# Two joints of a transformer kernel in another order: weight splits and norm steps around a feed forward and a compressed projection

## The chip, the cores and the metric

The kernel is one program on one core of a Trainium2 chip. The metric is the device time of a whole launch in microseconds (us), the median of several runs. Beside the timed runs there is one profiled execution, and all times of single instructions come from it.

## The reference, cut to what matters

512 tokens of width 1024 go through two transformer blocks. All matmuls are in float32. What bears on the change:

```python
# first block: ... attention and gates give `merged`
mix_out = merged @ w_out                       # output product 1
h = h + rms_norm(mix_out, norm_mix_post)
n2 = rms_norm(h, norm_mlp_pre)
hid = square(relu(n2 @ w_up))                  # feed forward 1
h = h + rms_norm(hid @ w_down, norm_mlp_post)
# second block, layer 0: latent attention
hn = rms_norm(x, norm_mix[0])
cq = rms_norm(hn @ w_dq, q_norm)               # compressed queries, 384 wide
dkv = hn @ w_dkv                               # 256 compressed + 32 shared key columns
ckv = rms_norm(dkv[..., :256], kv_norm)
q = cq @ w_uq ; kv = ckv @ w_ukv               # then 16 heads of attention, w_o, feed forward 2
# layer 1: mLSTM mixer, w_o, feed forward 3
```

The two feed forwards and the output products of the second block have no norm behind them (`h = h + y`).

## The kernel before, in words

**Products in three passes.** Each float32 product is made of three matmuls in a reduced format (`mm3`, lines 82 to 84): hi*hi, hi*lo and lo*hi. So every operand is split into a hi part (ScalarE copies it to the narrower format) and a lo part (VectorE subtracts hi from the original).

**Weight units.** The weights come in units of up to 128x2048, in one fixed order (`plan_units`). A unit passes through two slots: SyncE loads it into `raw_weights` when VectorE has split the unit two before it (`load_unit`); ScalarE makes `weights_hi` (`split_hi`, L305, or `hi` in the feed forward, L1328) once it has landed and TensorE is through with the unit two before; VectorE makes `weights_lo` (`split_lo`, L311, or `lo`, L1423). TensorE waits for the lo part. The unit of a feed forward is 256 columns of `w_up` (two per step) or 512 of `w_down` (two per step), eight steps (`NF`); the compressed projections have three: 256 columns of the queries, the other 128 with 32 of the shared key, and 256 key-value columns.

**Order.** Nothing is scheduled by a planner. Each engine runs its queue in the order written in the code and waits on counting semaphores. The stages (`out_product`, `ffn`, `mla_down`, `mla`) follow each other without a barrier in one block.

**Norms.** The 512 tokens are four tiles of 128. Between two stages the residual is normed in two halves, tiles 0 and 1, then 2 and 3 (`norm_halves`). Per tile ScalarE sums squares (L962) and takes a root (L967); per half VectorE takes the reciprocal (L978) and scales the tiles (L981), TensorE transposes them (`turned`, L989, 16 transposes), ScalarE makes the hi part with the norm's gain from PSUM (L999, eight pieces of 128x256), VectorE the lo part (L1009). Where the product before has a norm behind it (`gain` given: output product 1 and feed forward 1), there is a second set of steps: VectorE adds the last partial product (L1467), ScalarE sums squares (L1380, or L1091 from PSUM) and takes roots (L1386, L1097), VectorE multiplies by the gain (L1470, or L1137) and updates the residual (`updated`, L1482, L1149). In these cases the next norm sums over the whole width at once (`whole=True`).

**The end of a feed forward on TensorE.** In the last step tokens 0 and 1 are finished in both column halves, then tokens 2 and 3; the first half's transposes stand ahead of the last group of matmuls. The next stage begins with the products of tiles 0 and 1 and has the second half's transposes a little later (in `ffn` behind `up_half(1, 0, 0)`, in `mla_down` behind `second(0)`).

**The compressed projections** (`mla_down`): TensorE makes unit one for tiles 0 and 1 (`first`), unit two for tile 0 (`second`), the transposes, then the rest; unit three for four tiles; and twelve transposes of the normed queries (L1588). ScalarE squares the query part from PSUM (L1602), splits units, squares the key-value part (L1609), makes the queries' hi (L1615); VectorE norms the queries (L1629), the key-values (L1638), and makes the queries' lo (L1642). The attention begins with a query product that waits for that lo.

## Time and profile before

| | before |
|---|---|
| median of 3 runs (lowest to highest) | 2203.77 us (2203.49 to 2205.46) |
| profiled execution, its own time | 2203.86 us |
| its span | 2202.1 us |
| TensorE busy (PE) | 2089.7 us, 95%, 11129 matmuls |
| VectorE busy (DVE) | 947.9 us, 43% |
| ScalarE busy (ACT) | 846.4 us, 38% |
| mean granted TensorE clock | 0.979 |

PE is TensorE's matmul queue, PEld its weight loads, DVE VectorE, ACT ScalarE, POOL GpSimd. Matmuls overlap, so the distance between their starts, not their length, is their price. A granted clock (PEclk) of 1.00 is the 2.4 GHz level, 0.50 the 1.2 GHz level. A row of a timeline is: start in us from the span's start, us until its end, engine, line, operation, what it writes and reads, the shape, the count of merged instructions, and in brackets how long the engine stood still just before and who ended that. Merged rows run from the first start to the last end.

### The profile page before, as it was taken

What the parts mean: (1) busy time and instruction counts of PE and PEld (TensorE: products, weight loads), DVE (VectorE), ACT (ScalarE), POOL (GpSimd) and SP (SyncE); (2) the same over time, 40 slices, a digit from 0 to 9 for tenths busy, and PEclk for the clock granted to TensorE, in tenths of its full rate; (3) what the DMA queues carried; (4) which work ended last, traced back from release to release, by engine and by line L of the source; (5) the groups of instructions that cost most, each with busy time, mean ns of one, the idle gap of its engine ahead of it and who ended that gap; (6) DMA issues with size and microseconds to landing.
All of it is one profiled execution on the core that took longest, in us unless ns stands there. A gap on an engine that the chain in (4) does not pass through costs nothing.

```text
span 2202.1 us, 26914 instructions
## 1 busy us (share of the span) xinstructions
PE 2089.7 (95%) x11129; PEld 1788.5 (81%) x11129; DVE 947.9 (43%) x1316; ACT 846.4 (38%) x1228; POOL 8.8 (0%) x20
## 2 busy tenths in 40 slices
PE   5799999999999999888889999999999999999999
PEld 5688888789888888686778988888877789888887
DVE  3545543334543344536554444334443344443343
ACT  3322332323533333536564433333454444333332
POOL 0000000000000000010000000000000000000000
PEclk9999999999999999988899999999999999999999
DMA  5232221223233333110011233223222212322322
GB/s 188 68 87 68 67 68 58 96 95 98 77 96 95 95 97 101 63 42 21 25 36 42 74 113 97 95 95 95 83 72 77 77 45 72 115 95 95 95 95 79
DMA packets 169800, 178.97 MB, mean 81 GB/s; under 512 B 6753, under 2 KB 139438, under 8 KB 169586
## 3 DMA queue, kind: packets, MB, share of 16 engines
q1 hardware_dynamic: 168280, 176.58, 25.5%
q8 instruction: 65, 1.06, 0.2%
q10 hardware_dynamic: 922, 1.09, 0.2%
q14 instruction: 21, 0.17, 0.0%
q0 software_dynamic: 512, 0.07, 0.0%
HBM read 174.50 MB, written 2.10 MB: 80 GB/s over the span
## 4 chain that ended last, share of the span: by engine, by line
PE 71%; DVE 6%; ACT 4%; issue 1%; ACTq 0%; DVEq 0%
PE psum L82 22%; PE psum L84 22%; PE psum L83 22%; DVE weights_lo L311 1%; PE psum L1790 1%; PE psum L1765 1%; PE psum L2177 1%; DVE weights_lo L1423 1%; PE psum L989 1%; ACT weights_hi L305 1%; PE psum L1780 1%; DVE scratch L1965 1%; ACT weights_hi L1328 0%; PE psum L1750 0%; ACT scratch L962 0%
## 5 line engine op out<-in xcount | busy, mean ns | idle before, releaser
L82 PE MATMUL psum<-norm_T_hi,weights_hi 128*128 128x512 f32 (+1 forms) x1440 | 540.4, 375 | 19.8 <-PEq L491 7.8
L84 PE MATMUL psum<-norm_T_hi,weights_lo 128*128 128x512 f32 (+1 forms) x1440 | 535.5, 372 | 0.0
L83 PE MATMUL psum<-norm_T_lo,weights_hi 128*128 128x512 f32 (+1 forms) x1440 | 535.3, 372 | 0.0
L82 PE MATMUL psum<-weights_hi,act_T_hi 128*128 128x512 f32 (+2 forms) x976 | 370.3, 379 | 14.8 <-DVE act_T_lo L1642 6.0
L84 PE MATMUL psum<-weights_hi,act_T_lo 128*128 128x512 f32 (+2 forms) x976 | 367.1, 376 | 0.0
L83 PE MATMUL psum<-weights_lo,act_T_hi 128*128 128x512 f32 (+2 forms) x976 | 367.1, 376 | 0.0
L82 PEld LDWEIGHTS psum<-norm_T_hi,weights_hi 128*128 128x128 f32 x1440 | 273.3, 190 | 70.3 <-issue 15.2
L84 PEld LDWEIGHTS psum<-norm_T_hi,weights_lo 128*128 128x128 f32 x1440 | 273.0, 190 | 46.9
L83 PEld LDWEIGHTS psum<-norm_T_lo,weights_hi 128*128 128x128 f32 x1440 | 273.4, 190 | 45.5
L1328 ACT ACTIVATE weights_hi<-raw_weights 128x2048 fp32r<-128x2048 f32 x93 | 177.5, 1909 | 342.2 <-PE psum L84 342.2
L1423 DVE TENSOR_TENSOR weights_lo<-raw_weights,weights_hi 128x2048 fp32r<-128x2048 f32 x93 | 213.2, 2293 | 106.7 <-ACT weights_hi L1328 106.7
L311 DVE TENSOR_TENSOR weights_lo<-raw_weights,weights_hi 128x2048 fp32r<-128x2048 f32 (+3 forms) x74 | 156.2, 2112 | 181.9 <-ACT weights_hi L305 179.2
L82 PEld LDWEIGHTS psum<-weights_hi,act_T_hi 128*128 128x128 f32 x976 | 186.8, 191 | 49.7 <-issue 7.2
L84 PEld LDWEIGHTS psum<-weights_hi,act_T_lo 128*128 128x128 f32 x976 | 186.5, 191 | 31.4
L83 PEld LDWEIGHTS psum<-weights_lo,act_T_hi 128*128 128x128 f32 x976 | 186.9, 191 | 30.8
L82 PE MATMUL psum<-weights_hi,norm_T_hi 128*128 128x256 f32 (+2 forms) x672 | 194.3, 289 | 17.0 <-DVE weights_lo L311 9.2
L1431 DVE TENSOR_TENSOR act_T_lo<-scratch,act_T_hi 128x512 fp32r<-128x512 f32 x96 | 66.4, 692 | 323.9 <-ACT act_T_hi L1339 323.9
L83 PE MATMUL psum<-weights_lo,norm_T_hi 128*128 128x256 f32 (+2 forms) x672 | 191.7, 285 | 0.0
L84 PE MATMUL psum<-weights_hi,norm_T_lo 128*128 128x256 f32 (+2 forms) x672 | 191.6, 285 | 0.0
L305 ACT ACTIVATE weights_hi<-raw_weights 128x2048 fp32r<-128x2048 f32 (+3 forms) x74 | 130.9, 1769 | 101.0 <-PE psum L84 90.4
L1335 ACT ACTIVATE scratch<-psum 128x512 f32<-128x512 f32 x96 | 57.5, 599 | 278.5 <-PE psum L84 278.5
L82 PEld LDWEIGHTS psum<-weights_hi,norm_T_hi 128*128 128x128 f32 x672 | 132.0, 196 | 20.1 <-DVE weights_lo L311 10.0
(256 smaller groups left out, 1958.7 us busy)
## 6 DMA issues: line engine op xcount, KB each, us to landing
raw_weights<-in_ffn_w_dram SPq DMA_DIRECT2D x64, 1024.0 KB, 5.2
raw_weights<-in_w_in_dram SPq DMA_DIRECT2D x36, 512.0 KB, 4.2
raw_weights<-in_w_up_dram SPq DMA_DIRECT2D x16, 1024.0 KB, 5.6
raw_weights<-in_w_down_dram SPq DMA_DIRECT2D x16, 1024.0 KB, 4.9
raw_weights<-in_w_in_dram SPq DMA_DIRECT2D x12, 1024.0 KB, 5.1
raw_weights<-in_mlstm_w_in_dram SPq DMA_DIRECT2D x8, 1024.0 KB, 5.2
raw_weights<-in_w_out_dram SPq DMA_DIRECT2D x4, 1024.0 KB, 5.4
raw_weights<-in_mla_w_o_dram SPq DMA_DIRECT2D x4, 1024.0 KB, 5.8
```

Of the source, the lines that this page charges most:

```text
L82: pe.matmul(out, ah, bh, start=start, stop=False)
L83: pe.matmul(out, ah, bl, start=False, stop=False)
L84: return pe.matmul(out, al, bh, start=False, stop=stop)
L305: act.activation(WH[:, u % 2, 0:c], RAW[:, u % 2, 0:c], ACT.Copy).then_inc(w_hi, 1)
L311: dve.tensor_tensor(WL[:, u % 2, 0:c], RAW[:, u % 2, 0:c], WH[:, u % 2, 0:c].bitcast(F32), SUB).then_inc(w_lo, 1)
L989: mm = pe.transpose(PS[:, bank, q * P:q * P + P], XN[:, t, k * P:k * P + P], IDENT[:, :])
L1328: act.activation(WH[:, u % 2, :], RAW[:, u % 2, :], ACT.Copy).then_inc(w_hi, 1)
L1335: act.activation(HS[:, f, :], PS[:, up_banks[f], :], ACT.Relu).then_inc(fr.sem, 1)
L1423: dve.tensor_tensor(WL[:, u % 2, :], RAW[:, u % 2, :], WH[:, u % 2, :].bitcast(F32), SUB).then_inc(w_lo, 1)
L1431: dve.tensor_tensor(AL[:, f, :], HS[:, f, :], AH[:, f, :].bitcast(F32), SUB).then_inc(fl.sem, 1)
L1765: pe.matmul(PS[:, b, c:c + w], QT[:, n % 2, t * P:t * P + P], KT[:, n % 2, 0:w], start=True, stop=True).then_inc(sc.sem, 1)
L1780: mm = pe.transpose(PS[:, 3 + q % 2, (i % 4) * P:(i % 4) * P + P], SB[:, i * P:i * P + P], IDENT[:, :])
```

## The change

Only the two stages with a gain and their successors change their order: output product 1 into feed forward 1, and feed forward 1 into the compressed projections.

- `normed` leaves tile 3 out where `whole` is set; a new step `normed_last` scales it on ScalarE, and `turned` waits for both.
- At the end of `out_product` with a gain, the split of the feed forward's second unit stands behind `updated(1)` and `rooted(3)`; `ffn` no longer has it (`whole_in`). On ScalarE that is the same place, on VectorE it is ahead of `normed`.
- At the end of `ffn` with a gain, ScalarE splits the next unit and makes the first half's hi pieces ahead of all squares of tiles 2 and 3; VectorE does the lo part and the lo pieces ahead of the multiplies, and splits the unit after it behind `updated(1)`.
- In `mla_down`, unit three is split ahead of the four squares of the query part; TensorE's twelve transposes of the queries move ahead of the last token tile of unit three; the hi and lo of the queries move ahead of the squares of tiles 2 and 3 and of the key-values' norm.
- A parameter `ahead=0` of `out_product`, three unused or new semaphores, and a count are bookkeeping.

```diff
@@ norm_halves @@
                     for t in (2 * h, 2 * h + 1):
-                        dve.tensor_scalar(XN[:, t, :], X[:, t, :], rstd[:, t:t + 1], None, MUL).then_inc(xnc.sem, 1)
+                        if not (whole and t == 3):
+                            dve.tensor_scalar(XN[:, t, :], X[:, t, :], rstd[:, t:t + 1], None, MUL).then_inc(xnc.sem, 1)
+
+                @staticmethod
+                def normed_last(act):
+                    act.wait_ge(rsc.sem, rsc.at(2))
+                    act.activation(XN[:, 3, :], X[:, 3, :], ACT.Copy, scale=rstd[:, 3:4]).then_inc(xlc.sem, 1)
 
                 @staticmethod
                 def turned(pe, h):
-                    pe.wait_ge(xnc.sem, xnc.at(2 * h + 2))
+                    pe.wait_ge(xnc.sem, xnc.at(3 if whole and h else 2 * h + 2))
+                    if whole and h:
+                        pe.wait_ge(xlc.sem, xlc.at(1))
                     for b, bank in enumerate((banks_a, banks_b)[h]):
@@ out_product, scalar @@
                     rooted(3)
+                    split_hi(act, u0 + 5)
                 else:
@@ out_product, vector @@
                     updated(1)
+                    split_lo(dve, u0 + 5)
                 else:
@@ ffn, scalar @@
                 if whole_in:
-                    hi(act, 0, 0)
                     for t in (2, 3):
                         came_in(t)
                         norm.last_sum(act, t)
+                    norm.normed_last(act)
                 else:
@@ ffn, scalar @@
                         nxt.last_sum(act, t)
+                    split_hi(act, u0 + 4 * NF)
+                    nxt.hi(act, 0)
                     squared(0, 2)
-                    split_hi(act, u0 + 4 * NF)
                     squared(0, 3)
                     squared(1, 2)
                     rooted(2)
-                    nxt.hi(act, 0)
                     squared(1, 3)
                     rooted(3)
+                    split_hi(act, u0 + 4 * NF + 1)
                 elif nxt:
@@ ffn, vector @@
                 norm.normed(dve, 1)
-                lo(dve, 0, 0)
+                if not whole_in:
+                    lo(dve, 0, 0)
                 norm.lo(dve, 1)
@@ ffn, vector @@
                     dve.wait_ge(stage_ld.sem, stage_ld.at(16))
-                    for h in range(2):
-                        t = 2 * h
-                        add(0, t)
-                        add(0, t + 1)
-                        if h:
-                            split_lo(dve, u0 + 4 * NF)
-                        for b in range(2):
-                            if b:
-                                add(1, t)
-                                if h:
-                                    nxt.lo(dve, 0)
-                                add(1, t + 1)
-                            dve.wait_ge(acc.sem, acc.at(8 * (NF - 1) + added[b][t + 1]))
-                            scaled(b, t)
-                            scaled(b, t + 1)
-                            if b == 0:
-                                mean(h)
-                        updated(h)
-                        if h == 0:
-                            nxt.normed(dve, 0)
+                    def landed(b, t):
+                        dve.wait_ge(acc.sem, acc.at(8 * (NF - 1) + added[b][t]))
+                        scaled(b, t)
+
+                    add(0, 0)
+                    add(0, 1)
+                    landed(0, 0)
+                    landed(0, 1)
+                    mean(0)
+                    add(1, 0)
+                    add(1, 1)
+                    landed(1, 0)
+                    landed(1, 1)
+                    updated(0)
+                    nxt.normed(dve, 0)
+                    add(0, 2)
+                    add(0, 3)
+                    split_lo(dve, u0 + 4 * NF)
+                    nxt.lo(dve, 0)
+                    landed(0, 2)
+                    landed(0, 3)
+                    mean(1)
+                    add(1, 2)
+                    add(1, 3)
+                    landed(1, 2)
+                    landed(1, 3)
+                    updated(1)
+                    split_lo(dve, u0 + 4 * NF + 1)
                 else:
@@ mla_down @@
                 for t in range(NT):
+                    if t == 3:
+                        pe.wait_ge(xn.sem, xn.at(NT))
+                        for k in range(3):
+                            for q in range(NT):
+                                mm = pe.transpose(PS[:, banks[k], q * P:q * P + P], CQ[:, q, k * P:k * P + P], IDENT[:, :])
+                            mm.then_inc(tp.sem, 1)
                     group_N(pe, u0 + 2, 0, 256, 256, KD,
...
-                pe.wait_ge(xn.sem, xn.at(NT))
-                for k in range(3):
...
             @block.scalar
             def _(act):
-                split_hi(act, u0 + 1)
+                def squared(t):
...
                 for t in (2, 3):
                     act.wait_ge(res_in.sem, res_in.at(t + 1))
                     norm.last_sum(act, t)
+                norm.normed_last(act)
                 norm.hi(act, 1)
+                split_hi(act, u0 + 2)
                 for t in range(NT):
                     act.wait_ge(gemm, cq_done[t])
-                    if t == 2:
-                        split_hi(act, u0 + 2)
...
                 split_hi(act, u0 + 3)
-                for t in range(NT):
...
-                act.wait_ge(ms.sem, ms.at(2))
-                act.activation(root[:, 4:8], m0[:, 4:8], ACT.Sqrt).then_inc(rt.sem, 1)
+                squared(0)
+                squared(1)
                 for k in range(3):
...
+                squared(2)
+                squared(3)
+                act.wait_ge(ms.sem, ms.at(2))
+                act.activation(root[:, 4:8], m0[:, 4:8], ACT.Sqrt).then_inc(rt.sem, 1)
...
             def _(dve):
                 norm.normed(dve, 1)
-                split_lo(dve, u0 + 1)
                 norm.lo(dve, 1)
+                split_lo(dve, u0 + 2)
                 dve.wait_ge(sq.sem, sq.at(4))
                 dve.tensor_scalar(m0[:, 0:4], s0[:, 0:4], 1.0 / QR, EPS, MUL, ADD).then_inc(ms.sem, 1)
-                split_lo(dve, u0 + 2)
                 dve.wait_ge(rt.sem, rt.at(1))
...
+                split_lo(dve, u0 + 3)
+                for k in range(3):
+                    dve.wait_ge(th.sem, th.at(k + 1))
+                    dve.scalar_tensor_tensor(in_place(AL[:, k, :]), by_tile(PS[:, banks[k], :]), col(C_MISC, k),
...
                 dve.wait_ge(sq.sem, sq.at(8))
...
-                split_lo(dve, u0 + 3)
...
-                for k in range(3):
-                    dve.wait_ge(th.sem, th.at(k + 1))
...
```

VectorE, from output product 1 into feed forward 1 (L1149 or L1161 the residual update, L1423 or L314 the lo part of unit 1, L981 or L985 the scaled tiles, L1009 or L1020 the transposed norm's lo). Before:

```order
L1149 SCALAR_TENSOR_TENSOR residual<-scratch,small,residual 128x1024 x2
L1426 UNCONDITIONAL_BRANCH
L978 RECIPROCAL small<-small 128x2
L981 TENSOR_SCALAR scratch<-residual,small 128x1024 x2
L1423 TENSOR_TENSOR weights_lo<-raw_weights,weights_hi 128x2048
L1009 SCALAR_TENSOR_TENSOR norm_T_lo<-psum,gain_columns,norm_T_hi 128x256 x8
```

Now:

```order
L1161 SCALAR_TENSOR_TENSOR residual<-scratch,small,residual 128x1024 x2
L314 TENSOR_TENSOR weights_lo<-raw_weights,weights_hi 128x2048
L1440 UNCONDITIONAL_BRANCH
L981 RECIPROCAL small<-small 128x2
L985 TENSOR_SCALAR scratch<-residual,small 128x1024
L1020 SCALAR_TENSOR_TENSOR norm_T_lo<-psum,gain_columns,norm_T_hi 128x256 x8
```

The lo part of the unit moved from behind the scaled tiles to right behind the update, and one scaled tile is gone.

ScalarE, end of feed forward 1 (L967 or L970 the next norm's root, L1380 or L1393 the squares, L305 or L308 the hi part of the next unit, L999 or L1010 the transposed norm's hi). Before:

```order
L967 ACTIVATE small<-small 128x1
L1380 ACTIVATE scratch,small<-scratch 128x512
L305 ACTIVATE weights_hi<-raw_weights 128x2048
L1380 ACTIVATE scratch,small<-scratch 128x512 x2
L1386 ACTIVATE small<-small 128x1
L999 ACTIVATE norm_T_hi<-psum,gain_columns 128x256 x8
L1380 ACTIVATE scratch,small<-scratch 128x512
L1386 ACTIVATE small<-small 128x1
```

Now:

```order
L970 ACTIVATE small<-small 128x1
L308 ACTIVATE weights_hi<-raw_weights 128x2048
L1010 ACTIVATE norm_T_hi<-psum,gain_columns 128x256 x8
L1393 ACTIVATE scratch,small<-scratch 128x512 x3
L1399 ACTIVATE small<-small 128x1
L1393 ACTIVATE scratch,small<-scratch 128x512
L1399 ACTIVATE small<-small 128x1
L308 ACTIVATE weights_hi<-raw_weights 128x1280
```

The split and the eight hi pieces stand ahead of all four squares of tiles 2 and 3.

ScalarE in the compressed projections (L1602 or L1630 squares of the query part, L1609 or L1619 of the key-value part, L1615 or L1639 the queries' hi). Before:

```order
L999 ACTIVATE norm_T_hi<-psum,gain_columns 128x256 x8
L1602 ACTIVATE scratch,small<-psum 128x384 x2
L305 ACTIVATE weights_hi<-raw_weights 128x2048
L1602 ACTIVATE scratch,small<-psum 128x384 x2
L1605 ACTIVATE small<-small 128x4
L305 ACTIVATE weights_hi<-raw_weights 128x1152
L1609 ACTIVATE scratch,small<-psum 128x256 x4
L1612 ACTIVATE small<-small 128x4
L1615 ACTIVATE act_T_hi<-psum,gain_columns 128x4x128 x3
```

Now:

```order
L990 ACTIVATE scratch<-residual,small 128x1024
L1010 ACTIVATE norm_T_hi<-psum,gain_columns 128x256 x8
L308 ACTIVATE weights_hi<-raw_weights 128x2048
L1630 ACTIVATE scratch,small<-psum 128x384 x4
L1633 ACTIVATE small<-small 128x4
L308 ACTIVATE weights_hi<-raw_weights 128x1152
L1619 ACTIVATE scratch,small<-psum 128x256 x2
L1639 ACTIVATE act_T_hi<-psum,gain_columns 128x4x128 x3
L1619 ACTIVATE scratch,small<-psum 128x256 x2
L1643 ACTIVATE small<-small 128x4
```

The 2048-wide split stands ahead of all squares, the queries' hi between the two pairs of key-value squares, and the scaled tile (L990) ahead of the hi pieces.

## Rows read from the trace of the kernel before

**Rows 1.** Waits over the span: total us, times, longest us
```profile
PE psum L82 <- DVE weights_lo L311: 16.3, 10, 4.2
```

**Rows 2.** Timeline of TensorE, joint A: start, us, instruction, idle time before
```profile
568.78 0.58 PE L82 MATMUL psum<-norm_T_hi,weights_hi 128*128 128x256 f32 x1 [4.86 <-DVE weights_lo L1423]
...
573.89 1.91 PE L989 MATMUL psum<-ident,scratch 128*128 128x128 f32 x16
575.56 0.36 PE L82 MATMUL psum<-norm_T_hi,weights_hi 128*128 128x256 f32 x1
...
590.57 0.50 PE L82 MATMUL psum<-weights_hi,act_T_hi 128*128 128x512 f32 x1 [0.39 <-DVE weights_lo L1423]
```

**Rows 3.** Timelines of ScalarE and VectorE, joint A
```profile
559.75 1.90 ACT L1328 ACTIVATE weights_hi<-raw_weights 128x2048 fp32r<-128x2048 f32 x1
...
564.90 0.17 DVE L978 RECIPROCAL small<-small 128x2 f32<-128x2 f32 x1 [1.72 <-ACT small L967]
...
566.44 2.29 DVE L1423 TENSOR_TENSOR weights_lo<-raw_weights,weights_hi 128x2048 fp32r<-128x2048 f32 x1
```

**Rows 4.** Stretches: busy PE, PEld, DVE, ACT, POOL; PEclk; DMA share; GB/s
```profile
514.00:516.00 2.00, 0.53 (x4) 0.53 (x5) 1.42 (x1) 0.00 (x0) 0.00 (x0) 1.00 0.00 0
...
925.00:929.00 4.00, 3.37 (x17) 3.40 (x18) 3.97 (x10) 2.30 (x6) 0.00 (x0) 0.57 0.13 44
...
937.00:945.00 8.00, 7.86 (x37) 7.87 (x38) 0.77 (x3) 1.55 (x4) 0.00 (x0) 0.50 0.30 76
```

**Rows 5.** ScalarE's groups by shape: busy us, mean ns, idle us before
```profile
L436 ACT ACTIVATE scratch<-residual,small 128x1024 f32<-128x1024 f32 x2 | 2.2, 1140 | 0.2 <-DVE small L450 0.2
```

**Rows 6.** Timeline of TensorE, stretch B
```profile
925.63 0.55 PE L82 MATMUL psum<-weights_hi,norm_T_hi 128*128 128x256 f32 x1 [5.44 <-DVE norm_T_lo L1009]
...
937.14 0.50 PE L82 MATMUL psum<-weights_hi,norm_T_hi 128*128 128x160 f32 x1 [4.21 <-DVE weights_lo L311]
...
962.71 0.56 PE L82 MATMUL psum<-weights_hi,norm_T_hi 128*128 128x256 f32 x1 [3.07 <-DVE weights_lo L311]
...
983.25 0.69 PE L82 MATMUL psum<-weights_hi,act_T_hi 128*128 128x384 f32 x1 [5.95 <-DVE act_T_lo L1642]
...
988.83 0.42 PE L82 MATMUL psum<-weights_hi,act_T_hi 128*128 128x384 f32 x1
...
992.16 0.47 PE L82 MATMUL psum<-weights_hi,act_T_hi 128*128 128x512 f32 x1
```

**Rows 7.** Timeline of ScalarE, stretch B
```profile
913.46 0.30 ACT L967 ACTIVATE small<-small 128x1 f32<-128x1 f32 x1
...
916.67 1.90 ACT L305 ACTIVATE weights_hi<-raw_weights 128x2048 fp32r<-128x2048 f32 x1
...
923.75 3.01 ACT L999 ACTIVATE norm_T_hi<-psum,gain_columns 128x256 fp32r<-128x256 f32 x8
...
957.00 1.92 ACT L305 ACTIVATE weights_hi<-raw_weights 128x2048 fp32r<-128x2048 f32 x1 [7.84 <-PE psum L84]
```

**Rows 8.** Timeline of VectorE, stretch B
```profile
918.60 2.29 DVE L311 TENSOR_TENSOR weights_lo<-raw_weights,weights_hi 128x2048 fp32r<-128x2048 f32 x1 [2.00 <-ACT weights_hi L305]
...
924.61 3.23 DVE L1009 SCALAR_TENSOR_TENSOR norm_T_lo<-psum,gain_columns,norm_T_hi 128x256 fp32r<-128x256 f32 x8 [1.84 <-ACT norm_T_hi L999]
...
928.47 1.29 DVE L1470 TENSOR_TENSOR scratch<-scratch 128x512 f32<-128x512 f32 x2
...
929.87 2.48 DVE L1482 SCALAR_TENSOR_TENSOR residual<-scratch,small,residual 128x1024 f32<-128x1024 f32 x2
...
935.60 1.49 DVE L311 TENSOR_TENSOR weights_lo<-raw_weights,weights_hi 128x1280 fp32r<-128x1280 f32 x1
```

**Rows 9.** Timelines of three engines: compressed queries turned and split
```profile
975.83 1.47 PE L1588 MATMUL psum<-ident,scratch 128*128 128x128 f32 x12
...
977.22 3.02 ACT L1615 ACTIVATE act_T_hi<-psum,gain_columns 128x512 fp32r<-128x512 f32 x3
...
980.03 3.17 DVE L1642 SCALAR_TENSOR_TENSOR act_T_lo<-psum,gain_columns,act_T_hi 128x512 fp32r<-128x512 f32 x3
```

More of the change, by code:

```diff
@@ L282, in build @@
         gate = count("gate_rows")
+        oth = count("head_pairs_hi")
+        qsc = count("query_scales")
+        n_xl = count("norm_last_scaled")
         drained = count("heads_gated")
@@ L403, in _ @@
                     dve.tensor_copy(COLS[:, :, :].rearrange("p a k -> p (a k)")[:, 0:NCOL], PS[:, 0, 0:NCOL]).then_inc(v1.sem, 1)
-            param.passed(32)
+            param.passed(32); cleared.passed(1)
             stage_ld.passed(10 * 16)
@@ L1027, in halves, with out_product @@
             return x[:, t, 512 * b:512 * b + 512]
-        def out_product(block, name, gain, banks, nxt, srch, srcl, ready, early, freed=None):
+        def out_product(block, name, gain, banks, nxt, srch, srcl, ready, early, freed=None, ahead=0):
             u0 = at[name]
@@ L1098, in rooted @@
                                    bias=pm[:, t:t + 1]).then_inc(qr.sem, 1)
-                for j in range(3):
+                for j in range(ahead, 3):
                     split_hi(act, u0 + j + 1)
@@ L1154, in add @@
                     dve.tensor_tensor(x, psum(b, t), x, ADD).then_inc(res.sem, 1)
-                for j in range(3):
+                for j in range(ahead, 3):
                     split_lo(dve, u0 + j + 1)
```

16 lines of the change are left out of this document (6 added, 10 removed).

## The prediction

> **What bounds the kernel.** I read the table of engines and the slices first: TensorE is busy for nearly the whole span, VectorE and ScalarE for less than half. So ScalarE's and VectorE's work costs nothing by itself; it counts only where TensorE stands still for it. The list of waits for TensorE is the second view: on top stands VectorE's lo half of a weight unit (L311), 16.3 us in ten waits, the longest 4.2 [rows 1]. Third, the timelines of the three engines at the places that the diff touches. There are two: the joint from the first output product into the first feed forward (554 to 592 us, joint A), and the stretch from the end of that feed forward through the compressed projections into the latent attention (900 to 1000 us, stretch B). Everything else keeps its order: `ahead` is given by no call and stays 0, and the other output products and feed forwards go through the `gain is None` and `whole=False` paths. No matmul, split or DMA is added or removed.
>
> **Joint A.** TensorE stood still for 4.86 us, until 568.78, when the lo half of feed forward unit 1 was ready [rows 2]. On VectorE [rows 3] that split (2.29, from 566.44) stood behind the residual update, which ended at 564.90 - 1.72 = 563.18, a wait of 1.72 for ScalarE's root, the reciprocal and two scaled tiles (565.07 to 566.44, 0.7 each). Its hi half had been there since 559.75 + 1.90 = 561.65. Now it comes right behind the update: 563.15 + 2.29 = 565.4. TensorE resumes 3.35 us earlier.
>
> The second gain is the clock. The 24 matmuls behind the old wait took 573.89 - 568.78 = 5.11 us, 0.213 each; the 120 behind the transposes took 590.57 - 575.56 less a gap of 0.39, so 0.122 each [rows 2]. The granted clock was 0.50, the 1.2 GHz level, behind such waits [rows 4]. The wait that is left is 563.92 to 565.4, 1.5 us. From 514 to 516 TensorE stood still for as long (busy 0.53 of 2.00) and the clock was granted at 1.00 [rows 4]; so I take the 2.4 GHz level: 24 x 0.122 = 2.93, 2.2 us less. Sum: 5.5 us.
>
> What takes the place of the old wait? The transposes need all four normed tiles. The reciprocal now starts at 565.45, tile 2 is scaled by VectorE, tile 3 by ScalarE at 1.14 us [rows 5], the price of the same operation elsewhere in the kernel against 0.7 on VectorE, side by side: ready at 566.9. TensorE comes for them at 565.4 + 2.9 = 568.3. Hidden by 1.4 us; were that cover gone, the cost would be what lies over it, 0 to 1.14 us.
>
> **Stretch B, first unit.** Four waits lie here [rows 6]: 5.44, 4.21, 3.07 and 5.95 us. Before the first, ScalarE split the unit's hi half from 916.67, behind a square that waited for VectorE [rows 7], and made the eight transposed hi pieces only after two more squares, one more wait, a square and a root, from 923.75. Now the split follows the root that ends at 913.76. It may start then: its source is long landed, and the products that still need its slot end near 913 (24 matmuls of 512 columns, near 0.23 each, and 16 transposes lie between them and TensorE's stop at 920.19). So hi ends at 915.7. VectorE is free for lo at 918.60 - 2.00 = 916.60 [rows 8] and ends it at 918.9. The hi pieces take 3.01 us from about 916.1, as soon as the first bank is transposed; the lo pieces 3.23 us from 918.9 to 922.1, a pair each 0.81 us. TensorE is free at 925.63 - 5.44 = 920.19, finds the first pair (919.7), and uses a pair in 6 x 0.122 = 0.73 us. The wait of 5.44 is gone and 48 matmuls end at 926.0.
>
> **Second unit.** Its lo half started at 935.60, behind the update of tiles 2 and 3 (929.87) and two scaled tiles [rows 8]. The update depends on squares and sums that now come after the lo pieces: VectorE has two multiplies, a mean, two adds, two multiplies, six passes of 0.65 (two took 1.29) and the two small ones at 0.16 [rows 8], so 4.3 us: update from 926.4 to 928.9 instead of 929.87 to 932.35. ScalarE's four squares and two roots interleave and end with it. The split follows directly (1.49): TensorE's second unit starts at 930.4 instead of 937.14, **6.75 us** earlier. A wait of 926.0 to 930.4 = 4.4 us remains, as long as the old one, and I let it cost what the old one did: half level through 24 matmuls and 16 transposes, to about 945.6 [rows 4]. ScalarE's scaled tile is ready before these 24 matmuls end, as in A.
>
> **Third unit.** ScalarE started its hi half at 957.00, held by the wait for the third token tile's product. It now stands first and waits only for the fourth tile of unit one, 24 matmuls of 2.7 us earlier, near 954.3 in the old times: hi 956.2, lo (2.29) 958.5, before TensorE's old stop at 959.64. So the wait of **3.07** goes. The squares of the query part move behind it by up to 1.9 us; they were done long before they are needed. With no stop there, the slow start goes too: 96 matmuls took 975.83 - 962.71 = 13.12 us, at 0.122 each 11.7: **1.4 us**.
>
> **Into the attention.** The twelve transposes of the compressed queries now stand ahead of the last 24 matmuls of the unit. Before, TensorE ended them at 977.30 and stood until 983.25 for hi (3.02) and lo (3.17, from 980.03) [rows 9]. Now, in new times, the unit starts at 959.64 - 6.75 = 952.9, the transposes are reached after 72 x 0.122 = 8.8 at 961.7, take 1.35, and the last product ends at 966.0. Queries are normed by 956.9 (squares 953.6, mean, root, reciprocal, four tiles 2.6), 4.8 us of cover. Hi runs from 962.3, lo from 963.35 to 966.5. The query product starts at 966.55 against 983.25, 16.7 us earlier in all. Of the 5.95 us wait 0.6 remains, and the clock need not fall: 18 matmuls and 8 transposes took 988.83 - 983.25 = 5.58; the next 18 took 992.16 - 988.83 = 3.33 [rows 6], so with 0.8 for the transposes 4.13: **1.45 us**. Sum of B: 18.15.
>
> Behind that all engines keep their distances. Sixteen small copies of the shared key part start with the transposes, some 14.5 us earlier, and VectorE wants them 18 us earlier; that could hold VectorE for about a microsecond, in front of a 3.6 us idle stretch before its next split. I cost it at nothing; without that cover it is 0 to 1 us.
>
> Total: 5.5 + 18.15 = **23.7 us**. The profiled execution took 2203.86 (span 2202.10, 1.76 around it), so 2180.2; the median of the runs is 0.09 lower, so I say 2180.1.
>
> The clock is where a page bears on it. The Trainium skill, TensorE: Matmul & The Clock Gate, Part 1, says that the gate is checked on a free-running rhythm, so the same kernel can meet it at another phase. By that rule the 4.4 us wait may or may not be followed by the lower level, and the sum would be that of the first rival below where it is not. The trace bears out both: behind the 5.44 us wait the half level lasted only to about 928.7 (0.57 from 925 to 929), behind the shorter one of 4.21 it held 8 us [rows 4].
>
> **Rivals.**
> 1. The clock stays up over the second unit. 24 matmuls at 0.11 to 0.12 instead of 0.213 give 2.4, 16 transposes 575.56 - 573.89 = 1.67 [rows 2] instead of the 3.3 left of the 8.4 another 1.6: 4.0 more, 2176.1. For it: the 5.44 us wait was nearly over before the level fell. Against: the matmuls behind the other four long waits, 4.86, 4.21, 3.07 and 5.95, all started slow. Chance 0.14.
> 2. The third unit's hi half comes too late after all, since ScalarE waits in front of its squares. The 3.07 stays with its slow start (1.4) and the slow query product (1.45): 5.9 less, 2186.0. The margin is 1.1 us. Chance 0.12.
> 3. The diff acts only on paths that TensorE does not feel, or the attention behind takes the gain back (shared keys, its own waits): 2204. Against it, TensorE names these very steps as releasers. Chance 0.02.
> 4. Slower: the half level, once met at the second unit, does not end. After it, 120 matmuls would cost 0.096 more each (11.5), 96 another 0.091 (8.7), the transposes and the 18 query matmuls 3.7: 23.9, all of the gain. Six more groups at this level, 24 key-value matmuls at 0.43 for 0.23 and 18 queries, add 7: 2211. It decides from about 24 us lost, near 45 us of unbroken half level; the longest here, behind the 4.21, ended soon after 945. Chance 0.02.
>
> **Numbers.** Forecast 0.70, rivals as above. A measurement of this kernel can tell 0.2% (4.4 us) from no change. Forecast and rivals 1 and 2 are faster: 0.96; same 0.02; slower 0.02. The range takes in the first two rivals with their own errors, 2 us either way for the clock in the attention: 2174 to 2188.
>
> **What would show it.** In the new profile: a wait of about 1.5 us in place of 4.86 in joint A and no lower clock behind it; no wait ahead of the first compressed unit, about 4.4 ahead of the second, none ahead of the third; under 1 us ahead of the query product. ScalarE scales two tiles of 128x1024 more, VectorE two fewer. I am wrong if the waits shrink and the time does not, or if new waits on the scaled tiles or on the squares show at TensorE's transposes.

## The result and the profile after

| | before | after |
|---|---|---|
| median (lowest to highest) | 2203.63 us (2203.41 to 2205.46) | 2183.05 us (2181.51 to 2183.6) |
| span of the profiled execution | 2202.1 us | 2180.9 us |
| mean granted TensorE clock | 0.979 | 0.979 |

The ratio is 0.9903, 95% interval 0.989 to 0.9915: 20.6 us less. The forecast was 2180.1 us, 23.7 less. The time lies inside the range, 3 us off. Where these 3 us are is what most of the runs below ask. One execution of run 1 below took 2381.16 us at a granted clock of 0.838 and is left out of that run's figures.

**Joint A.** TensorE of the changed kernel, beside [rows 2]:

```profile
565.35 0.39 PE L82 MATMUL psum<-norm_T_hi,weights_hi 128*128 128x256 f32 x1 [1.53 <-DVE weights_lo L314]
...
568.33 1.91 PE L1000 MATMUL psum<-ident,scratch 128*128 128x128 f32 x16
569.99 0.36 PE L82 MATMUL psum<-norm_T_hi,weights_hi 128*128 128x256 f32 x1
...
585.01 0.50 PE L82 MATMUL psum<-weights_hi,act_T_hi 128*128 128x512 f32 x1 [0.39 <-DVE weights_lo L1437]
```

The wait is 1.53 us in place of 4.86, and the 24 matmuls behind it took 568.33 - 565.35 = 2.98 us in place of 5.11. VectorE and ScalarE, beside [rows 3], show why: the split (L314) now comes ahead of the reciprocal (L981), and tiles 2 and 3 are scaled side by side, the one on VectorE (L985), the other on ScalarE (L990), both done by 566.55, 1.8 us before TensorE comes for them. On the spot that is 3.33 + 2.13 = 5.5 us; the new kernel stood 0.1 us ahead already when its wait began (563.82 for 563.92).

```profile
563.01 2.28 DVE L314 TENSOR_TENSOR weights_lo<-raw_weights,weights_hi 128x2048 fp32r<-128x2048 f32 x1
565.21 0.15 DVE L981 RECIPROCAL small<-small 128x2 f32<-128x2 f32 x1
565.40 0.75 DVE L985 TENSOR_SCALAR scratch<-residual,small 128x1024 f32<-128x1024 f32 x1
```
```profile
565.40 1.15 ACT L990 ACTIVATE scratch<-residual,small 128x1024 f32<-128x1024 f32 x1 [0.62 <-DVE small L981]
```

**Stretch B.** TensorE, beside [rows 6] and the transposes of [rows 9]; the first row, the first unit's first matmul, has no wait:

```profile
914.34 0.28 PE L82 MATMUL psum<-weights_hi,norm_T_hi 128*128 128x256 f32 x1
...
924.33 0.34 PE L82 MATMUL psum<-weights_hi,norm_T_hi 128*128 128x160 f32 x1 [4.07 <-DVE weights_lo L314]
...
932.02 0.32 PE L82 MATMUL psum<-weights_hi,norm_T_hi 128*128 128x160 f32 x1
...
954.53 1.47 PE L1610 MATMUL psum<-ident,scratch 128*128 128x128 f32 x12
...
959.74 0.44 PE L82 MATMUL psum<-weights_hi,act_T_hi 128*128 128x384 f32 x1 [0.86 <-DVE act_T_lo L1661]
```

From 932.02 up to the wait of 0.86 us that ends at 959.74 TensorE has no wait at all; unit three starts inside, at 945.87. VectorE in the same stretch, beside [rows 8]: the split of unit one and the lo pieces run without a pause, and the split of unit two follows the update directly.

```profile
910.84 2.28 DVE L314 TENSOR_TENSOR weights_lo<-raw_weights,weights_hi 128x2048 fp32r<-128x2048 f32 x1
913.04 3.22 DVE L1020 SCALAR_TENSOR_TENSOR norm_T_lo<-psum,gain_columns,norm_T_hi 128x256 fp32r<-128x256 f32 x8
...
920.39 2.48 DVE L1497 SCALAR_TENSOR_TENSOR residual<-scratch,small,residual 128x1024 f32<-128x1024 f32 x2
922.79 1.49 DVE L314 TENSOR_TENSOR weights_lo<-raw_weights,weights_hi 128x1280 fp32r<-128x1280 f32 x1
```

**What came later.** The same matmul starts this much earlier in the changed kernel (start before less start after): second unit 937.14 - 924.33 = 12.8 us, third 962.71 - 945.87 = 16.8, query product 983.25 - 959.74 = 23.5, first matmul of the second query product, behind the first key-value product, 1001.16 - 976.12 = 25.0. At the end of the span it is 21.2. So 3.8 us of what stood at 976 us were handed back behind it, in stages whose code and order are the same. Matching matmuls tell where. At the last transposes of the attention, ahead of the output product, the lead is still 24.7:

```profile
1199.57 0.63 PE L1755 MATMUL psum<-ident,scratch 128*128 128x128 f32 x4 [0.68 <-DVE scratch L1975]
```
```profile
1174.92 0.63 PE L1782 MATMUL psum<-ident,scratch 128*128 128x128 f32 x4 [0.68 <-DVE scratch L2002]
```

In feed forward 2 it is 22.9 (1266.76 and 1243.88), in the mixer 21.7 (1705.58 and 1683.84), at output product 3 21.2 (1804.92 and 1783.75). The stretches show the clock there. Before (busy PE, PEld, DVE, ACT, POOL; PEclk; DMA share; GB/s):

```profile
1036.00:1056.00 20.00, 17.51 (x82) 14.23 (x83) 14.53 (x39) 10.19 (x23) 0.00 (x0) 0.66 0.10 31
1088.00:1108.00 20.00, 17.47 (x84) 14.38 (x85) 14.60 (x39) 10.38 (x24) 0.00 (x0) 0.66 0.17 54
1136.00:1160.00 24.00, 16.53 (x97) 13.77 (x98) 16.48 (x42) 14.02 (x30) 0.00 (x0) 0.86 0.00 1
1196.00:1208.00 12.00, 9.41 (x66) 8.80 (x66) 4.76 (x4) 4.31 (x3) 0.00 (x0) 0.86 0.15 46
1628.00:1640.00 12.00, 9.08 (x41) 6.98 (x42) 6.17 (x6) 5.54 (x7) 0.00 (x0) 0.86 0.61 176
1780.00:1796.00 16.00, 12.58 (x68) 10.81 (x67) 8.51 (x21) 5.90 (x14) 0.00 (x0) 0.89 0.00 0
```

After, the same six places of the program:

```profile
1008.00:1028.00 20.00, 16.16 (x57) 13.01 (x58) 13.34 (x30) 9.24 (x19) 0.00 (x0) 0.57 0.09 29
1060.00:1080.00 20.00, 17.02 (x65) 13.87 (x66) 13.31 (x31) 9.35 (x20) 0.00 (x0) 0.57 0.15 53
1112.00:1136.00 24.00, 21.71 (x100) 17.91 (x101) 16.27 (x41) 13.50 (x29) 0.00 (x0) 0.64 0.00 1
1176.00:1188.00 12.00, 10.00 (x60) 9.73 (x61) 5.28 (x3) 3.89 (x3) 0.00 (x0) 0.72 0.52 164
1604.00:1616.00 12.00, 8.47 (x31) 6.48 (x30) 7.39 (x7) 6.13 (x7) 0.00 (x0) 0.72 0.50 142
1756.00:1772.00 16.00, 12.58 (x53) 9.97 (x52) 8.45 (x24) 7.11 (x11) 0.00 (x0) 0.79 0.00 1
```

In all six the granted clock is lower than before. The first three lie in the attention, where it costs next to nothing in this profile, 0.4 us: TensorE waits there for VectorE in any case (for the rotation of queries and keys), and a slower approach only shortens that wait. The waits from 1000 to 1160 us show it, in one line of before and one of after (total, times, longest):

```profile
PE psum L1750 <- DVE scratch L1955: 8.6, 3, 5.3
```
```profile
PE psum L1777 <- DVE scratch L1982: 3.2, 3, 1.1
```

The last three lie at the start of output product 2, early in the mixer behind feed forward 2, and late in the mixer, where less covers it. 12 us at 0.72 in place of 0.86 is 1.7 us of clock more, 16 at 0.79 in place of 0.89 is 1.6: 5.0 in the three. The leads above fall by 1.8, 1.0 and 0.5 us around them, 3.3 in all, so the waits inside them cover the rest. The mean clock of the whole is 0.979 in both kernels: the change took four waits away and did not lessen the share of the lower level; that share moved.

### The profile page after: what moved, and what is told of

Same layout as the page of the kernel before. It is cut to its first block, busy times and chain, and to the rows that moved or that the text cites. A ratio compares the mean times of both kernels' runs of the same rounds, so it can differ in the third digit from the quotient of the medians.

```text
span 2180.9 us, 26916 instructions
## 1 busy us (share of the span) xinstructions
PE 2091.1 (96%) x11129; PEld 1789.5 (82%) x11129; DVE 946.2 (43%) x1314; ACT 848.9 (39%) x1230; POOL 8.8 (0%) x20
## 4 chain that ended last, share of the span: by engine, by line
PE 71%; DVE 6%; ACT 3%; issue 1%; ACTq 0%; DVEq 0%
PE psum L82 22%; PE psum L84 22%; PE psum L83 22%; DVE weights_lo L314 1%; PE psum L1817 1%; PE psum L1792 1%; PE psum L2204 1%; PE psum L1807 1%; DVE weights_lo L1437 1%; PE psum L1000 1%; DVE scratch L1992 1%; ACT weights_hi L308 0%; ACT weights_hi L1341 0%; PE psum L1777 0%; PE psum L2183 0%
## 5 line engine op out<-in xcount | busy, mean ns | idle before, releaser
L314 DVE TENSOR_TENSOR weights_lo<-raw_weights,weights_hi 128x2048 fp32r<-128x2048 f32 (+1 forms) x75 | 158.5, 2114 | 189.7 <-ACT weights_hi L308 187.0
L308 ACT ACTIVATE weights_hi<-raw_weights 128x2048 fp32r<-128x2048 f32 (+1 forms) x75 | 132.8, 1770 | 102.8 <-PE psum L84 92.0
```

Of the source, the lines that this page charges most:

```text
L308: act.activation(WH[:, u % 2, 0:c], RAW[:, u % 2, 0:c], ACT.Copy).then_inc(w_hi, 1)
L314: dve.tensor_tensor(WL[:, u % 2, 0:c], RAW[:, u % 2, 0:c], WH[:, u % 2, 0:c].bitcast(F32), SUB).then_inc(w_lo, 1)
```

## The experiments

All are compared with runs of the kernel before on the same chip; each gives its ratio with 95% interval.

**1. Joint A alone.** The end of the feed forward and the compressed projections are in the order of before; against the changed kernel:

```diff
@@ ffn, scalar @@
-                    split_hi(act, u0 + 4 * NF)
-                    nxt.hi(act, 0)
                     squared(0, 2)
+                    split_hi(act, u0 + 4 * NF)
                     squared(0, 3)
                     squared(1, 2)
                     rooted(2)
+                    nxt.hi(act, 0)
                     squared(1, 3)
                     rooted(3)
-                    split_hi(act, u0 + 4 * NF + 1)
...
@@ mla_down, vector @@
                 norm.normed(dve, 1)
+                split_lo(dve, u0 + 1)
                 norm.lo(dve, 1)
...
```

VectorE's end of the feed forward, unit three and the queries' transposes, hi and lo go back in the same way.

> The order of joint A alone (the end of output product 1 into the feed forward), with tile 3 of both norms still scaled by ScalarE; everything behind it in the order of before. Forecast's theory: the wait ahead of the second unit's matmuls shrinks from 4.86 to 1.5 us and the 24 matmuls behind it take 2.9 in place of 5.1 us, so 5.5 us less than before: 2198.1. Rival, the wait shrinks but the matmuls stay at the lower level: 3.3 less, 2200.3. Second rival, the gain is handed back at the clock's lower stretches further on, as some 4 us of the full change were: 2 to 6 us less, with joint A itself 5.5.

Measured: 2198.45 for 2204.33, ratio 0.9969 (0.9958 to 0.998): 5.9 less by the medians, 4.4 to 9.3 by the interval. The seven runs spread from 2194.45 to 2201.06, so this agrees with the 5.5 forecast and does not measure it to half a us. TensorE does:

```profile
566.63 0.39 PE L82 MATMUL psum<-norm_T_hi,weights_hi 128*128 128x256 f32 x1 [1.54 <-DVE weights_lo L314]
...
569.61 1.91 PE L1000 MATMUL psum<-ident,scratch 128*128 128x128 f32 x16
```

Wait 1.54, and 2.98 us for the 24 matmuls, as in the changed kernel: both halves of this term stand. The run also keeps tile 3 on ScalarE in the second norm, which takes 0.6 us off the wait ahead of the second compressed unit (3.62 for 4.21); so it is joint A and a little more. From the second query product, where it is 4.5 us ahead of before, to the end, where it is 4.4, it hands nothing back.

**2. The change without joint A.**

```diff
@@ out_product, scalar and vector @@
                     rooted(3)
-                    split_hi(act, u0 + 5)
...
                     updated(1)
-                    split_lo(dve, u0 + 5)
@@ ffn, scalar and vector @@
                 if whole_in:
+                    hi(act, 0, 0)
...
-                if not whole_in:
-                    lo(dve, 0, 0)
+                lo(dve, 0, 0)
```

> The whole change without joint A: the split of the feed forward's second unit is back behind the norm. Theory: wait of 4.86 us and the slow 24 matmuls are back, 5.5 us more than the changed kernel, 2188.6, and 15.1 less than before. If the two parts add up, this gain and that of joint A alone make the 20.6 of the whole; if the clock's phase takes a share of its own, they do not, by up to 4 us.

Measured: 2186.8 for 2204.33, ratio 0.9922 (0.9908 to 0.9935): 3.8 more than the changed kernel's 2183.05, 3.4 more than run 3 on the same chip, not 5.5. The expectation had forgotten that tile 3 stays on ScalarE. The split stands behind the scaled tiles again, so it gains what VectorE no longer does, 0.65 us, and this time the lower level ended inside the 24 matmuls (4.33 us for 5.11). Wait and matmuls together are 4.0 us longer than in the changed kernel:

```profile
567.73 0.58 PE L82 MATMUL psum<-norm_T_hi,weights_hi 128*128 128x256 f32 x1 [4.21 <-DVE weights_lo L1436]
...
572.06 1.91 PE L1000 MATMUL psum<-ident,scratch 128*128 128x128 f32 x16
```

**3. Tile 3 on VectorE.** Both calls of `normed_last` and the wait for it are gone:

```diff
@@ norm_halves @@
-                        if not (whole and t == 3):
-                            dve.tensor_scalar(XN[:, t, :], X[:, t, :], rstd[:, t:t + 1], None, MUL).then_inc(xnc.sem, 1)
+                        dve.tensor_scalar(XN[:, t, :], X[:, t, :], rstd[:, t:t + 1], None, MUL).then_inc(xnc.sem, 1)
```

> The changed kernel with tile 3 of both norms scaled by VectorE as before. Theory: the tile is wanted only 1.4 us (joint A) and more (stretch B) after it is ready in either way, so no change at the joints: 2183.0, within 0.5. Rival: the transposes wait for VectorE, 0.3 to 0.7 us at each joint, up to 1.4 us more.

Measured: 2183.45 for 2204.33, ratio 0.9905 (0.989 to 0.992); no difference from the changed kernel, and its transposes in joint A have no wait. Where the split comes ahead of the norm, moving the tile gains nothing; where it stands behind it, as in run 2, it shortens the wait by 0.65.

**4. The changed kernel once more.**

> The changed kernel once more, unaltered, with a profile of its own. If the stretches of lower clock hang on what TensorE did before them, all twelve come at the same places to 4 us and the span repeats to 0.5 us. If they hang on something that runs beside the kernel, single stretches are longer, shorter or absent, and the runs spread by steps of 1 to 3 us at a granted clock from 0.978 to 0.985.

Measured: 2183.23 for 2203.3, ratio 0.9907 (0.9891 to 0.9922). The profiled span is 2182.5, 1.6 longer than the first, and stretches have changed their clock. Two of them, 0.86 and 1.00 here; in the first profile 1176 to 1188 stood at 0.72, and in 1136 to 1160 the level was full:

```profile
1136.00:1160.00 24.00, 22.15 (x130) 17.54 (x128) 10.51 (x38) 12.89 (x35) 0.00 (x0) 0.86 0.13 45
1176.00:1188.00 12.00, 8.18 (x67) 7.66 (x66) 5.70 (x4) 4.31 (x3) 0.00 (x0) 1.00 0.19 60
```

So the clock of a stretch is not fixed by the program alone. The Trainium skill, TensorE: Matmul & The Clock Gate, Part 1, has the gate checked on a free-running rhythm; the two profiles agree, 0.72 and 1.00 in one stretch of one program. They don't explain the 3 us by chance, though: none of the eight runs of the changed kernel came under 2181.5.

The same 4 us are handed back here, but elsewhere. The second query product starts at 977.50, 23.7 us ahead of before, and at the end of the attention the lead is only 20.4:

```profile
1179.14 0.63 PE L1782 MATMUL psum<-ident,scratch 128*128 128x128 f32 x4 [0.68 <-DVE scratch L2002]
```

So 3.2 us went inside the attention, in its last part, where TensorE no longer waits for VectorE: from 1138 to 1146 the clock is 0.57, and in the same part of the first profile, 1137 to 1145, it is 1.00. Behind that only 0.8 more is lost.

**5. The compressed queries last.** Transposes, hi and lo stand where they stood before; of ScalarE's part:

```diff
@@ mla_down, scalar @@
                 squared(0)
                 squared(1)
-                for k in range(3):
-                    act.wait_ge(tp.sem, tp.at(k + 1))
-                    act.activation(in_place(AH[:, k, :]), ...)
                 squared(2)
                 squared(3)
                 act.wait_ge(ms.sem, ms.at(2))
                 act.activation(root[:, 4:8], m0[:, 4:8], ACT.Sqrt).then_inc(rt.sem, 1)
+                for k in range(3):
+                    act.wait_ge(tp.sem, tp.at(k + 1))
+                    act.activation(in_place(AH[:, k, :]), ...)
```

> The changed kernel with the compressed queries' transposes back behind the last token tile of unit three, and their hi and lo back behind the key-values' norm. Theory: the wait ahead of the query product goes from 0.86 back to 5.95 us and the 18 matmuls behind it start at the lower level: 5.1 + 1.45 = 6.6 more than the changed kernel, 2189.6. Rival, the attention behind has slack and hands some back: 2 to 4 more. The clock further on may add or take 2.

Measured: 2189.66 for 2203.3, ratio 0.9936 (0.9923 to 0.995): 6.4 more than the changed kernel's 2183.23 on the same chip. The wait ahead of the query product is 5.94 again. The term, 5.1 + 1.45, is right in the time.

**6. Unit three late.**

```diff
@@ mla_down, scalar @@
                 norm.hi(act, 1)
-                split_hi(act, u0 + 2)
                 for t in range(NT):
                     act.wait_ge(gemm, cq_done[t])
+                    if t == 2:
+                        split_hi(act, u0 + 2)
@@ mla_down, vector @@
                 norm.lo(dve, 1)
-                split_lo(dve, u0 + 2)
                 dve.wait_ge(sq.sem, sq.at(4))
                 dve.tensor_scalar(m0[:, 0:4], ...)
+                split_lo(dve, u0 + 2)
```

> The changed kernel with unit three's split back between the squares of the query part. Theory: the wait of 3.07 us ahead of unit three and its slow start of 1.4 are back: 4.5 more than the changed kernel, 2187.5. Rival: with the second unit early the hi half finds its product done and half of the wait stays away: 1.5 to 2.5 more, 2185.

Measured: 2184.01 for 2203.3, ratio 0.9913 (0.9898 to 0.9928): 0.8 more than the changed kernel, and its four runs, 2183.53 to 2185.02, overlap with that one's. Yet the wait is back in full:

```profile
949.35 0.58 PE L82 MATMUL psum<-weights_hi,norm_T_hi 128*128 128x256 f32 x1 [3.07 <-DVE weights_lo L314]
```

From the second unit's start (923.85) to the query product (964.71) it takes 40.86 us, in the repeat of run 4 36.40 (924.73 to 961.13): 4.5 us more. What was lost by 965 came back behind it: the clock of the three stretches in the attention is higher than in the first profile, the waits for VectorE there are long again, and the stretch at 1176 is at 0.86 (0.72).

```profile
1008.00:1028.00 20.00, 16.05 (x77) 12.35 (x78) 15.31 (x40) 11.95 (x26) 0.00 (x0) 0.74 0.00 0
1060.00:1080.00 20.00, 15.27 (x69) 11.17 (x69) 14.77 (x32) 12.37 (x26) 0.00 (x0) 0.72 0.00 1
1112.00:1136.00 24.00, 16.18 (x96) 13.48 (x95) 16.11 (x41) 14.25 (x31) 0.00 (x0) 0.86 0.00 1
1176.00:1188.00 12.00, 9.41 (x67) 8.80 (x66) 5.05 (x4) 4.31 (x3) 0.00 (x0) 0.86 0.19 56
```
```profile
PE psum L1778 <- DVE scratch L1983: 8.4, 3, 5.3
```

Its mean clock is 0.982, the changed kernel's 0.978 and 0.979: 0.003 to 0.004 of 2182 us, 6.5 to 8.7 us of full clock less lost. How far each profile is ahead of before, in us, shows that this kernel hands nothing back (the profiles differ from that of before by up to 1.2 us ahead of joint A already, so what counts is the change along a row):

| profile | second query product | end of the attention | feed forward 2 | span |
|---|---|---|---|---|
| changed kernel | 25.0 | 24.7 | 22.9 | 21.2 |
| changed kernel, run 4 | 23.7 | 20.4 | 20.5 | 19.6 |
| unit three late, run 6 | 20.1 | 20.3 | 20.3 | 20.3 |
| joint A alone, run 1 | 4.5 | 4.5 | 4.4 | 4.4 |

So this term of the forecast was right at its place, 4.5 us, and worth 0.8 in the whole.

**7 and 8. Work added.** Every transpose of the compressed queries is made twice, or three times, into the same place:

```diff
                         for k in range(3):
-                            for q in range(NT):
+                            for q in list(range(NT)) * 2:
```

> The changed kernel with every one of the twelve transposes of the compressed queries made twice, into the same place: work of 1.35 us more on TensorE near 955 us, nothing else altered. It moves all that follows by 1.35 us. Theory, the 3.9 us that the changed kernel loses behind 1176 us are a matter of where the lower clock falls: the time changes by something else than 1.35, and the stretches near 1180, 1610 and 1765 us are of another length. Rival, they are a fixed cost of the change: 1.35 more, 2184.4, with the same stretches.

> As the kernel with every one of the twelve transposes made twice, but three times: 2.7 us more of TensorE's work near 955 us. Work made twice had cost nothing that could be measured (2183.0 for 2183.2). If the delay is added to the end, 2185.9; if what follows is set by where the lower clock falls among VectorE's own waits in the attention, anything from 2182 to 2187, and the stretches there are of another length.

Measured: 2183.0 for 2203.3, ratio 0.9906 (0.9891 to 0.9921), and 2182.8 for 2204.72, ratio 0.9902 (0.9887 to 0.9917). Neither 1.35 nor 2.7 us of TensorE's time shows in the whole. Half of the expectation was wrong: the wait of 0.86 us ahead of the query product took the first part of the delay, so that this started only 0.5 and 1.4 us later than in the repeat of run 4 (961.67 and 962.52 for 961.13). The rest went with the clock: with three times, the stretch from 976 to 984 is at 1.00, where the repeat has 0.79:

```profile
976.00:984.00 8.00, 4.85 (x28) 4.88 (x29) 6.27 (x6) 5.04 (x8) 0.00 (x0) 1.00 0.37 89
```

Of the matmuls of the second query product, the first starts 1.65 us later than in the repeat (979.15 for 977.50), the seventeenth 0.1 (982.02 for 981.93). With two times, the attention takes the delay: behind it, at the wait shown in run 4, this kernel stands at 1179.18, the repeat at 1179.14. The rival, a fixed cost that a delay adds to, falls.

**9. The end of the feed forward back.** The part of run 1's diff that concerns `ffn` and the second unit's split in `mla_down`, on both engines, with unit three and the queries left as changed.

> The changed kernel with the end of feed forward 1 and the second unit's split back in the order of before; joint A, unit three and the queries stay changed. Theory: the waits of 5.44 ahead of the first and 4.21 ahead of the second compressed unit are back; the changed kernel's TensorE stood 8.0 us further ahead behind these two than ahead of them, so 8 more, 2191.2. Rival, from what undoing unit three cost (0.9 where 4.5 was forecast): the attention hides part of the lower clock behind VectorE's waits of its own, and only 4 to 5 us come through, 2188.

Measured: 2188.67 for 2204.72, ratio 0.9931 (0.9917 to 0.9945): 5.4 to 5.6 more than the changed kernel's medians on other chips; counted as 16.1 less than before, where the changed kernel had 20.6 and 20.1, only 4.0 to 4.5. That is nearer to the rival's number than to the theory's. TensorE:

```profile
919.48 0.55 PE L82 MATMUL psum<-weights_hi,norm_T_hi 128*128 128x256 f32 x1 [5.44 <-DVE norm_T_lo L1020]
...
930.32 0.34 PE L82 MATMUL psum<-weights_hi,norm_T_hi 128*128 128x160 f32 x1 [2.85 <-DVE weights_lo L314]
```

From the transposes ahead of the first unit (909.31) to the second unit it takes 21.0 us, in the changed kernel 14.5 (909.86 to 924.33): 6.5 more, not 8. Of 4.21 us of wait 2.85 are back. VectorE scales one tile less ahead of the split, 0.7, and the 48 matmuls between the waits were slower, 8.0 us for 7.3, inside the time that VectorE needs. The spans differ by 5.8, and this profile was 0.5 ahead at those transposes, so 6.3 of the 6.5 are there at the end: that the attention hides a part, the rival's reason, is not what this profile shows. The theory failed already ahead of the attention.

**10 and 11. One step further.** The second unit's split no longer waits for the update of tiles 2 and 3, and the transposes that do are behind both tiles of that unit:

```diff
@@ ffn, scalar @@
                     squared(0, 3)
+                    split_hi(act, u0 + 4 * NF + 1)
                     squared(1, 2)
...
-                    split_hi(act, u0 + 4 * NF + 1)
@@ ffn, vector @@
                     nxt.lo(dve, 0)
+                    split_lo(dve, u0 + 4 * NF + 1)
...
                     updated(1)
-                    split_lo(dve, u0 + 4 * NF + 1)
@@ mla_down, tensor @@
                 second(0)
-                norm.turned(pe, 1)
                 second(1)
+                norm.turned(pe, 1)
```

> A step further than the change: the compressed projections' second unit is split ahead of the multiplies and the update of tiles 2 and 3 (hi half between ScalarE's squares, lo half right behind the lo pieces), and TensorE takes the transposes of tiles 2 and 3 behind second(1) instead of behind second(0). Theory: the wait of 4.07 us ahead of the second unit goes; in its place TensorE waits for the normed tiles 2 and 3, near 927.0, reaching them at 925.5, 1.5 us; some 3 to 5 us less than the changed kernel, 2178 to 2180. Rival: the update falls behind by the 1.5 us of the split and ScalarE's squares by another 1.4, so that the transposes wait 3 us or more and only 1 us or less is gained: 2182. It would be slower if the third unit's squares came late in turn.

> The kernel with the second unit split early once more, beside the next one on the same chip: 2177.3 as before, within 1.5.

Measured: 2177.32 for 2204.33, ratio 0.9873 (0.9858 to 0.9888), and again 2174.84 for 2204.72, ratio 0.9865 (0.9849 to 0.988). It beats both kernels, the changed one by 6 to 8 us.

```profile
927.87 2.84 PE L1000 MATMUL psum<-ident,scratch 128*128 128x128 f32 x16 [1.89 <-ACT scratch L990]
```

One wait of 1.89 in place of one of 4.07, and 2.84 us for the 16 transposes behind it, so at the lower level; the query product starts at 956.18 for 959.74, 3.6 us earlier. The rest goes with the clock: single runs lie at 2173.65 to 2179.42, those with a mean clock of 0.984 or 0.985 under 2175.5, those with 0.980 or 0.981 over 2178.5. Both profiles, spans 2177.6 and 2176.9 at 0.980, are of the longest runs, so where the shorter ones save is not shown.

**12. The transposes of the queries ahead of tile 2.** In run 10's kernel `if t == 3` becomes `if t == 2`.

> The kernel with the second unit split early, and the twelve transposes of the compressed queries ahead of the third token tile of unit three instead of the fourth. Theory: the normed queries are there 1.7 us before TensorE comes for them, hi and lo lie under 48 matmuls instead of 24, and the wait of 0.86 us ahead of the query product goes: 0.9 less, 2176.4. Rival: the normed queries are late and TensorE waits at the transposes for up to 0.9 us instead, no change; or the gain vanishes in the attention, as the 1.35 us of added work did.

Measured: 2176.99 for 2204.72, ratio 0.9875 (0.986 to 0.989), beside 0.9865 (0.9849 to 0.988) for run 11 on the same chip: no gain that can be told, though the wait of 0.86 is gone and the query product starts at 954.30. By its profile the gain is there at the query product; in the times the spread of run 11, 2173.65 to 2178.71, is larger than it. That fits the second half of the rival and does not prove it.

## Why the prediction was right, and where it was not

- **Joint A, 5.5.** Measured 5.5 on the spot (3.33 of the wait, 2.13 of the 24 matmuls); alone, 5.9 with a wide spread (run 1). The cover of the scaled tiles held, 1.8 us for 1.4 (runs 1, 3).
- **First unit.** The wait of 5.44 is gone, as said. The lo pieces ended at 916.2, in old times 921.8, for 922.1.
- **Second unit, 6.75.** Measured 12.81 - 5.57 = 7.2 at its start, with the wait 4.07 for 4.4. The 48 matmuls ahead of it ran at the full level (5.92 us for 7.30), so TensorE waited as long, since VectorE sets the end.
- **The clock over the second unit** was taken as unchanged. 24 matmuls and 16 transposes took 932.02 - 924.33 = 7.69 us for about 8.4, and the 120 matmuls up to unit three all ran at the full level. Third unit and this together: 16.84 - 12.81 = 4.0 at the unit's start, of which 3.07 is the wait and 1.0 is a quarter of rival 1.
- **Rival 2** did not come: the third unit's lo was there in time and unit three has no wait.
- **Into the attention, 5.35 and 1.4.** Measured 23.5 - 16.8 = 6.7 with the slow start; the wait left is 0.86 for 0.6. **The 18 query matmuls, 1.45:** 25.0 - 23.5 = 1.5. The order of the queries undone, 5.35 and 1.45 together, cost 6.4 (run 5).
- **Sum up to there:** 25.0 measured for 23.65, 0.1 of it from ahead of joint A. The terms as listed add up to 5.5 + 18.0; the 18.15 comes from the start times.
- **The step that failed** is "behind that all engines keep their distances". Of the 25.0 us, 3.8 were handed back behind it. In the first profile 3.3 of them went at three places that the change does not touch, each with 1.6 to 1.7 us more lost to the lower level; in the second, 3.2 of 4.1 went in the last part of the attention (run 4). "Everything else keeps its order" is right; to read it as "everything else keeps its time" left out that the clock granted there can change without any change of code.
- **Rival 3** named the attention as a place that takes gain back. In the first profile it took 0.4: its waits for VectorE, 3.2 us for 8.6, hid 5.4 us of slower matmuls. In the second it took 3.2. So it was right in kind; in size, it said all of the gain.
- **Luck:** the terms came out 1.4 us too small and the part behind them 3.8 too large, and the two partly cancel. The forecast is 3.0 off where the step that failed is worth 3.8.
- **The shared-key copies at 0 to 1 us** were rightly taken at nothing: the second query product has the same wait of 3.28 ahead of it as before (3.29).
- **Still open:** why the changed kernel hands 4 us back, in both of its profiles and at different places, and the one with unit three late, like joint A alone, nothing. Run 4 shows that the low stretches move between executions of one program, run 6 that a wait of 3 us far ahead goes with fewer of them in all four of its runs (0.981 and 0.982); what the clock looks at no run here tells.

## What to carry to other kernels

Where the waits of the bound engine name the releaser, walk that engine's queue backwards from the releasing instruction; what stands ahead of it and is wanted later is the gain, and each wait and its price came out within 0.5 us here, but for the 1.0 us of clock in the second unit. But price the sum by two ledgers: what is gained on the spot, and what the clock gives or takes further on, which for single steps of 1 to 5 us was as large as the step. A step of a few us at one place is worth keeping only if the whole, run alone and undone, shows it: here 4.5 us on the spot were 0.8 in the time, and 2.7 us of added work were nothing.

## What was not expected of the hardware

- The mean granted clock stayed at 0.979 while 17 us of TensorE's waits went away at the joints (3.3, 5.4, 0.1, 3.1 and 5.1), and rose to 0.982 when one wait of 3.07 us was put back.
- The lower level may be free. In front of VectorE's rotation of queries and keys TensorE arrived up to 4.3 us later with more of the 1.2 GHz level, waited 1.1 in place of 5.3 us, and kept its lead to 0.4 us (25.0 and 24.7). In the last part of the attention, where no such wait follows, the same level cost 3.2 us (run 4).
- Waits of 1.5 us in joint A were followed by the full level in all twelve profiles that have them. One of 1.50 ahead of output product 2 (1177.05 in the first profile, 1181.28 in the second) was followed by 0.72 and by 1.00 in 1176 to 1188, in one and the same program. One of 1.88 was followed by the full level in run 12 (16 transposes in 1.94 us), while the same wait in run 10 was followed by the lower one (2.84). Behind waits of 3 to 6 us the level was low for part of the work, but not for the same part: 24 matmuls took 5.11 us behind 4.86 and 4.33 behind 4.21. The length of a wait alone does not tell what follows.
